# Layer 0's values product with the values stationary on two column halves, two heads at a time, and queries turned at another place

## The reference

```python
def blocked_gqa(q, k, v):              # layer 0: 8 query heads, 2 key heads, head_dim 64
    ...
        s = jnp.einsum('bqkgd,bskd->bkgqs', qblk, k, preferred_element_type=jnp.float32) * scale
        pr = jax.nn.softmax(s, axis=-1).astype(v.dtype)
        return jnp.einsum('bkgqs,bskd->bqkgd', pr, v)
...
def blocked_diff_attention(q, k, v, lam):   # layer 1: 8 heads, two maps each, value width 128
    ...
        pr = jax.nn.softmax(s, axis=-1)
        w = (pr[:, 0] - lam * pr[:, 1]).astype(v.dtype)
        return jnp.einsum('bhqs,bshe->bqhe', w, v)
```

## Time and profile before

| | before |
|---|---|
| median of 3 runs | 3952.06 us (3947.37 to 3953.08) |
| the profiled execution | 3954.31 us, span 3952.5 us |
| PE busy | 3465.6 us, 88% of the span |
| PE weight loads | 3147.7 us |
| VectorE busy | 1406.2 us, 36% |
| ScalarE busy | 1155.3 us, 29% |
| mean granted clock | 0.925 of 2.4 GHz |

### The profile page before, as it was taken

How to read it: one execution, slowest core, us unless ns; L and a number is a source line. 1 busy time by engine, 2 the same in 40 slices (tenths; PEclk the granted TensorE clock), 3 DMA queues, 4 the chain that set the end, 5 groups by cost and what they waited for, 6 DMA issues and landing times. The chain is left out here.

```text
span 3952.5 us, 62078 instructions
## 1 busy us (share of the span) xinstructions
PE 3465.6 (88%) x23998; PEld 3147.7 (80%) x23998; DVE 1406.2 (36%) x2656; ACT 1155.3 (29%) x2467; POOL 203.4 (5%) x177
## 2 busy tenths in 40 slices
PE   6795988996899999999499888889895499999998
PEld 3445877886599999999478777777795499999997
DVE  1456335333600000000567576666734400000002
ACT  2353544532111111111337364553612011111111
POOL 0001000000000000000010101001000000000000
PEclk7897999998699999999799999989996699999999
DMA  8300001001978888886410010101013488888884
GB/s 316 94 19 19 1 3 60 1 27 31 357 274 279 276 276 276 276 277 227 139 41 1 7 35 7 35 7 62 1 32 128 150 280 279 280 279 279 279 279 151
DMA packets 319413, 577.24 MB, mean 146 GB/s; under 512 B 28997, under 2 KB 80906, under 8 KB 318730
## 3 DMA queue, kind: packets, MB, share of 16 engines
q1 hardware_dynamic: 309120, 541.24, 38.6%
q0 software_dynamic: 9216, 33.56, 4.3%
q10 hardware_dynamic: 906, 0.23, 0.0%
HBM read 526.10 MB, written 48.90 MB: 145 GB/s over the span
## 5 line engine op out<-in xcount | busy, mean ns | idle before, releaser
L1659 PE MATMUL psum<-moeh_xe,moe_w 128*128 128x144 f32 x8192 | 1015.6, 287 | 2.2 <-ACT moeh_xe L1694 2.2
L1659 PEld LDWEIGHTS psum<-moeh_xe,moe_w 128*128 128x128 f32 x8192 | 1010.2, 191 | 3.0 <-ACT moeh_xe L1694 3.0
L1675 PE MATMUL psum<-moeh_hid,moe_w 128*128 128x144 f32 x4096 | 531.6, 287 | 1.4 <-DVE moeh_hid L1734 1.4
L1675 PEld LDWEIGHTS psum<-moeh_hid,moe_w 128*128 128x128 f32 x4096 | 514.3, 190 | 6.5 <-issue 4.7
L1734 DVE TENSOR_TENSOR moeh_hid<-moe_act,psum 128x144 f32<-128x144 f32 x256 | 77.9, 304 | 1088.7 <-ACT moe_act L1703 1088.7
L851 PE MATMUL psum<-attn_w_hi,attn_hs 128*128 128x256 f32 (+2 forms) x1440 | 377.0, 347 | 94.0 <-DVE attn_w_lo L1094 83.8
L851 PEld LDWEIGHTS psum<-attn_w_hi,attn_hs 128*128 128x128 f32 x1440 | 259.6, 194 | 125.4 <-DVE attn_w_lo L1094 85.4
L1703 ACT ACTIVATE moe_act<-psum 128x144 f32<-128x144 f32 x256 | 74.6, 291 | 936.1 <-PE psum L1659 936.1
L1180 DVE TENSOR_REDUCE attn_neg_max<-psum 128x1 f32<-128x1280 f32 (+1 forms) x216 | 292.7, 1355 | 112.2 <-PE psum L896 111.5
L924 PE MATMUL psum<-attn_v,attn_pt 128*128 128x64 f32 (+1 forms) x2592 | 317.0, 277 | 9.1 <-DVE attn_o L1204 3.4
L924 PEld LDWEIGHTS psum<-attn_v,attn_pt 128*128 128x128 f32 x2592 | 300.3, 192 | 28.6 <-ACT attn_pt L963 20.5
(11 more groups left out here) (226 smaller groups left out, 3445.3 us busy)
## 6 DMA issues: line engine op xcount, KB each, us to landing
moe_w<-in_l_w_gate SPq DMA_DIRECT2D x64, 2048.0 KB, 9.1
moe_w<-in_l_w_up SPq DMA_DIRECT2D x64, 2048.0 KB, 13.6
moe_w<-in_l_w_down SPq DMA_DIRECT2D x64, 2048.0 KB, 9.6
ada_w<-in_l_ada_w SPq DMA_DIRECT2D x36, 1024.0 KB, 13.8
ada1s_w<-in_l_ada_w SPq DMA_DIRECT2D x12, 1024.0 KB, 9.7
x_saved_dram<-region SPq DMA_DIRECT2D x2, 4608.0 KB, 13.6
region<-x_saved_dram SPq DMA_DIRECT2D x2, 4608.0 KB, 14.8
out_w<-in_l_w_out SPq DMA_DIRECT2D x16, 512.0 KB, 4.0
```

Of the source, the lines that this page charges most:

```text
L1659: last = pe.matmul(m.psum[:, at:at + ROWS], mm.w[2 * (f // 4) + i][:, k, col:col + P], mm.xe[:, k, :], start=(k == 0), stop=(k == KB - 1))
L1675: last = pe.matmul(m.psum[:, at:at + ROWS], mm.w[4 + n // 4][:, f, (n % 4) * P:(n % 4 + 1) * P], mm.hid[:, f, :], start=(f == 0), stop=(f ...
```

## The change

In layer 0 the product of values is turned round. The values of a key tile (64 columns) are stationary and the turned probabilities of 128 queries move. Two units (two heads of the same tile) are done together: one writes PSUM partitions 0 to 63, the other 64 to 127, so their result is 128 rows of the transposed output and VectorE copies it straight into `cat`. `turn_out` falls away in layer 0. Since the reciprocal now belongs to a column and not to a row of the result, VectorE multiplies the probabilities by it ahead of the turning, in place, 1280 columns a unit; PE's transposes wait for that (`mixed`). `pt` holds two units side by side. The turning of a unit's probabilities comes two positions behind instead of one (`lag`). In both layers the parts of a position stand in another order; the queries' `stage` comes behind the scores of the position, in layer 0 one position later, and in layer 1 behind the second scores. VectorE's own loop keeps its order.

```diff
     e = [put(f"e{i}", [P, KEYS]) for i in range(3)]
-    pt = [put(f"pt{i}", [P, KEYS]) for i in range(2)]
+    if l == 0:
+        pt = [put(f"pt{i}", [P, KT, 2, P]) for i in range(2)]
+    else:
+        pt = [put(f"pt{i}", [P, KEYS]) for i in range(2)]
     o_at = put.pos[0]
...
     turns_k = KT + 1
-    TURNS = turns_k + 2 * NT + 3 * (units - per_tile) + per_tile + 6
+    TURNS = turns_k + 2 * NT + 3 * (units - per_tile) + per_tile + (0, 6)[l]
+    nvalues = (units // 2, units)[l]
+    stage_step = (1, 0)[l]
+    lag = (2, 1)[l]
+    values_after = lambda u: (u - 4) // 2 if l == 0 and u % 2 == 0 and u >= 4 else u - 2 if l == 1 and u >= 2 else None
     turn_bank = lambda n: (6 + n % 2) * BANK
...
             make["scores"](0, i)
-        for u in range(units + 2):
-
+        for u in range(units + lag + 1):
+
+            if l == 1 and u + 1 < units:
+                make["scores"](u + 1, 0)
+            if lag <= u < units + lag:
+                make["turn_probs"](u - lag, 0)
+            if l == 0 and values_after(u) is not None:
+                make["values"](values_after(u))
             if u + 1 < units:
-                make["scores"](u + 1, 0)
-            if u % per_tile == 0 and u // per_tile + 1 < NT:
+                make["scores"](u + 1, maps - 1)
+            if u % per_tile == stage_step and u // per_tile + 1 < NT:
                 make["stage"](u // per_tile + 1)
-            if 1 <= u <= units:
-                make["turn_probs"](u - 1, 0)
-            if u + 1 < units and maps == 2:
-                make["scores"](u + 1, 1)
-            if 1 <= u <= units:
-                make["turn_probs"](u - 1, 1)
-            if u >= 2:
-                make["values"](u - 2)
-        make["turn_out"]()
+            if lag <= u < units + lag:
+                make["turn_probs"](u - lag, 1)
+            if l == 1 and values_after(u) is not None:
+                make["values"](values_after(u))
+        if l == 1:
+            make["turn_out"]()
...
                         if what == "output":
-                            pe.wait_ge(s["o_read"], j * units + count)
+                            pe.wait_ge(s["o_read"], j * nvalues + count)
                         else:
...
                     _, _, tiles = key_span(u)
-                    pe.wait_ge(s["expd"], j * nmaps + (u + 1) * maps)
-                    if l == 1:
-                        pe.wait_ge(s["mixed"], j * units + (u + 1))
+                    pe.wait_ge(s["mixed"], j * units + (u + 1))
                     src = e[u % 3]
...
+                def values_turned(v):
+
+                    _, _, tiles = key_span(2 * v)
+                    pe.wait_ge(s["turn_read"], j * TURNS + probs_at[2 * v + 1])
+                    at = next_bank(output=v)
+                    for i, kt in enumerate(tiles):
+                        for c in range(2):
+                            last = pe.matmul(m.psum[64 * c:64 * c + 64, at:at + P], vt[:, kt, :], pt[v % 2][:, i, c, :],
+                                             start=(i == 0), stop=(i == len(tiles) - 1))
+                    last.then_inc(s["pv_done"], 1)
+
                 def values(u):
+                    if l == 0:
+                        return values_turned(u)
                     _, _, tiles = key_span(u)
...
                 def turn_out():
-                    if l == 0:
-                        pe.wait_ge(s["o_read"], j * units + units)
                     for b in range(0, NT, 4):
-                        if l == 1:
-                            pe.wait_ge(s["o_normed"], j * 2 + (1 if b + 4 <= NORM_PARTS[0][1] else 2))
+                        pe.wait_ge(s["o_normed"], j * 2 + (1 if b + 4 <= NORM_PARTS[0][1] else 2))
                         for p in range(2):
...
                 def turn_out():
-                    if l == 1:
-                        square_out(units - 1)
-                        act.wait_ge(s["x_saved"], 16)
+                    square_out(units - 1)
+                    act.wait_ge(s["x_saved"], 16)
                     for b in range(0, NT, 4):
...
                             out = cat[:, ds(j * 2 + p, 1), b * P:(b + n) * P].rearrange("p o t -> p (o t)")
-                            read_turn(out, n * P, scale=m.subln[:, 0:1] if l == 1 else None)
+                            read_turn(out, n * P, scale=m.subln[:, 0:1])
...
                     dve.reciprocal(inv[:, n:n + maps], sums[:, n:n + maps])
-                    if l == 1:
-                        lo, hi, _ = key_span(u)
-                        dve.drain()
+                    lo, hi, _ = key_span(u)
+                    dve.drain()
+                    if l == 0:
+                        probs = e[u % 3][:, 0:hi - lo]
+                        dve.tensor_scalar(probs, probs, inv[:, n:n + 1], None, ALU.mult).then_inc(s["mixed"], 1)
+                    else:
                         dve.tensor_scalar(ratio[:, u:u + 1], sums[:, n:n + 1], inv[:, n + 1:n + 2], m.neg_lambda[:, 0:1],
...
                     at = out_bank[u]
+                    dve.wait_ge(s["pv_done"], j * nvalues + (u + 1))
                     if l == 0:
-                        dve.drain()
-                    dve.wait_ge(s["pv_done"], j * units + (u + 1))
+                        dst = cat[:, ds(j * 2 + u % 2, 1), (u // 2) * P:(u // 2 + 1) * P].rearrange("p o q -> p (o q)")
+                        dve.tensor_copy(dst, m.psum[:, at:at + P]).then_inc(s["o_read"], 1)
+                        return
                     c = (u % per_tile) * dv
...
                         norm_out(0)
-                    if u >= 2:
-                        read_out(u - 2)
+                    if values_after(u) is not None:
+                        read_out(values_after(u))
                 dve.drain()
...
                     norm_mean(1)

```

More of the change, by code:

```diff
@@ L745, in group @@
             def group(j, last):
-                wait_value(m, sp, s["pv_done"], j * units)
+                wait_value(m, sp, s["pv_done"], j * nvalues)
                 for t in range(PT_TILES):
@@ L986, in project @@
                     if t == 0:
-                        act.wait_ge(s["pv_done"], j * units)
+                        act.wait_ge(s["pv_done"], j * nvalues)
                         split_tokens(0)
@@ L1024, in turn_probs @@
                     _, _, tiles = key_span(u)
-                    if u >= 2 and part == 0:
+                    if l == 1 and u >= 2 and part == 0:
                         act.wait_ge(s["pv_done"], j * units + (u - 1))
+                    if l == 0 and u % 2 == 0 and u >= 4 and part == 0:
+                        act.wait_ge(s["pv_done"], j * nvalues + (u // 2 - 1))
                     for b in turn_parts(len(tiles), part):
                         n = min(4, len(tiles) - b)
-                        read_turn(pt[u % 2][:, b * P:(b + n) * P], n * P)
+                        if l == 0:
+                            read_turn(pt[(u // 2) % 2][:, b:b + n, u % 2, :], n * P,
+                                      groups_of=("p (n t) -> p n t", dict(t=P)))
+                        else:
+                            read_turn(pt[u % 2][:, b * P:(b + n) * P], n * P)
                     if part < maps and u + 2 < units:
```

## The result

The kernel after the change takes 3978.12 us (median of 4 runs, 3976.05 to 3981.33), the kernel before on the same chip 3951.72 (4 runs). The ratio is 1.0069, with a 95% interval of 1.0052 to 1.0087: slower by 26 us. The forecast was 3972 (3942 to 4034), slower with a chance of 0.70.

What follows compares the result with a forecast made beforehand. PE's own work in program order was taken to set layer 0, PE's work and copy waits layer 1. -9 (layer 0) + 23 (layer 1) + 6 (clock) = +20 on 3952 gave 3972 us, range 3942 to 4034.

Steps and rivals of the forecast that it cites:

- the four column groups of adaLN: Nearest trace row for layer 0's new values: 16 records ran four abreast in 1.86 us; two abreast gave 2.42 per pair.
- rival B: Layer 0 values: the column halves take turns, 4.54 us a pair, +68 us, 4040 in all; chance 9%.
- the estimated 7 us more: Layer 0 values: with a floor of about 62 ns per record, a pair takes 2.63 us and the sum is higher.
- The chain: Layer 0: VectorE reads output only behind maximum, reciprocal and multiply, 3.1 us after the scores; PE stands 2.9 per pair.
- The 2.9 us stall eats the 2.1 us won on values: Layer 0 tiles: PE's wait for VectorE's read cancels the faster values; a tile takes 22.9 us against 22.73.
- Predicted -9: Layer 0 in sum: +2.4 for tiles, -3 for later turning, -8.2 for the dropped output turning, in us.
- where I had 5.2: Layer 0 group starts: first positions shorter because values begin two positions later, -2.6 us per group, two groups.
- the two rows: Clock evidence: granted clock fell to 0.80 near 374, stayed 1.00 at 2292; layer 0's stalls between them, costed at nothing.
- Rival C: Layer 0: the clock falls behind every second stall, half the work at 1.2 GHz, +61 us, 4033; chance 16%.
- 3.4 + 1.5 for the clock: Layer 1 group starts: fifth scores 3.4 us later behind query copies, then 1.5 for work at 1.2 GHz.
- 23 + 6 = 29: Layer 1 in sum: +23 us from longer tiles and later group starts, +6 from the lower clock at four starts.
- Rival A: Layer 1's later queries cost nothing and the clock holds, so only -9 us is left, 3943; chance 17%.

Runs made afterwards that it cites:

- e9_filled: The changed kernel with five unused PE products ahead of 28 of layer 0's waits for VectorE's read; 3960.16 us, ratio 1.0025.
- e4_l1_alone: The kernel before, with only layer 1's query turning moved behind the second scores; 3981.0 us, ratio 1.0071.
- e6_no_multiply: The changed kernel with layer 0's multiply cut from 1280 columns to one; 3955.85 us, ratio 1.0012.
- e5_read_mid: The changed kernel with VectorE's read of a layer 0 pair's output between maximum and reciprocal; 3926.88 us, ratio 0.9939.

## Why the prediction came out right, step by step

**Values.** 2.42 us per pair was predicted from the four column groups of adaLN, 2.33 measured; two abreast is borne out by the exchanged loops and the run in one half, and rival B is out. The Trainium skill, TensorE: Matmul & The Clock Gate, has in the section "Wait — 56ns, not 53.3ns?" a floor of about 62 ns for a MATMUL decoded by the sequencer. Here 40 records take 2.33, 58 ns each, which is under that floor, so the estimated 7 us more do not appear; whether the sequencer decoded these records no run shows.

**The multiply and the stall.** 0.93 predicted, 0.89 measured; stall 2.9 predicted, 2.60 measured; about 85 us in all predicted, 76.9 in the page (28 long stalls and four short ones). The chain was right, and both placements of the read and the cut multiply confirm its links one by one. "The 2.9 us stall eats the 2.1 us won on values" holds: at full clock a tile takes 22.6, where it took 22.73. VectorE's extra work was put at 55 us; the multiply takes 59.0, but all of VectorE only 45.4 more, partly because layer 0's output is read 36 times and not 72.

**Layer 0 in sum.** Predicted -9. At full clock (`e9_filled`) it is 439.1 - 455.3 = -16.2; with the clock as it fell, +0.8. So two terms were mis-sized in opposite directions. The first are the 7 us at full clock. Cut at VectorE's query casts, the starts of the two groups are 9.9 shorter (386.46 to 403.51 before, 383.41 to 395.48 in `e9_filled`), where I had 5.2; the twelve tiles behind them are together 1.0 shorter, where I had 1.8 more; the rest, 5.2 shorter, is as predicted (5.4). Why the starts gave twice as much was not taken apart. The second is the step that failed: "The 2.9 us stalls of layer 0 lie between the two rows; I cost them at nothing". The two rows were a 5-us gap, behind which the clock fell, and a shorter one, behind which it held. It does fall in the stalls, not behind each one but in about every second window, and costs 17 to 18 us. Rival C had the mechanism and three and a half times its size (+61), because it let the clock fall behind every second stall for half of PE's work.

**Layer 1.** The tile was predicted 0.33 longer, and is 0.49: +0.15 for the first after the start and +0.49 for each of the next five, 2.6 per group against 2.3. The start was predicted 3.4 + 1.5 for the clock, 4.9; the four groups show 4.8, 4.4, 3.8 and 5.0, with a 5.04 us gap where 5 was predicted. Together 7.1 per group, 28.4 in four. The whole layer shows 24.5: 1.2 of the difference is one tile of the kernel before that took 14.72 instead of 13.52, and 2.6 lie between the groups and behind the last one, not traced to a cause. `e4_l1_alone` shows 27.3. Predicted were 23 + 6 = 29. Rival A, layer 1 free, is out.

**The sum.** Predicted -9 + 29 = +20; the profiled pair shows +0.8 + 24.5 - 3.7 = +21.6, the medians +26.4. That the total came so near is in part luck: 17 us of clock left out, against 7 us too little saving in layer 0, 4 too much for layer 1, and 3.7 in parts that were not changed. The forecast's own range, 3959 to 3988, is also narrower than its bounds: added up plainly, they give 3953 to 3992. The measured 3978 lies in both. The measured 26.4 lies 5 above the trace's pair, and neither that nor the 3.7 in unchanged parts was traced to a cause. The change also turns the probabilities a position later and moves layer 0's queries; neither was run by itself, so their shares of layer 0's saving are not known.

What I did not see when I predicted is the size of what lay idle: the change's own parts are worth 96 us more once the read stands first. The prediction said that the saving was eaten, and not that a move of two lines would free it.

## What to carry to other kernels

When work is moved into an in-order queue, list for every shared buffer who reads it and what stands in front of that read on its own engine: here 0.28 us of copying, placed behind 2.4 us of other work, cost 96 us of 3978, and it could be cured from either engine's side. Copies that feed the first scores of a group belong ahead of the exp on ScalarE, since there is no other work for PE there yet: 21 us here, in four group starts. Cost a stall with the clock in mind: here stalls of some 80 us took another 17 in slower work behind them.

## What the runs showed of the hardware

- Two column halves with 64 stationary columns each run abreast when their products alternate: 0.058 us per record against 0.113 in one half and 0.103 in rows of ten. The order of two nested loops is worth 51 us in this kernel, 55 by the ratios.
- Unused work can pay: products that fill a wait made the kernel 18 us faster, since the granted clock stayed at 1.00. In the kernel after, with waits of 2.60 us twice a tile, it fell to 0.83 in the window from 410 to 420, and in `e6_no_multiply`, with waits of 2.02, to 0.83 in the windows from 480 to 520; in `e5_read_mid`, with waits of 1.56 at the same places, every 10-us window from 400 to 540 was at 1.00.
